# Order of two small products and of two vector steps in the second block of a two-block model

## What is computed

```
h_lat, h_ctx = rmsnorm(x) * (1 + sc1) + sh1, the same of ctx   # sh, sc, gt from silu(c) @ w_ada + b_ada
cols = h @ w_in                                                # latent attention, mLSTM, gates
q = rmsnorm(rmsnorm(c_q) @ w_uq); k, v from rmsnorm(c_kv) @ w_ukv   # 4 heads of 192, then a rotation
mla = softmax(q k^T * 192**-0.5) @ v                           # keys: 256 of ctx, then 256 of x
mlstm = both directions: sum over s of exp(level(t, s)) * (q.k) * v, divided by max(|den|, exp(-m))
x = x + gt1 * (concat(mla, mlstm) @ w_out)
h2 = rmsnorm(x) * (1 + sc2) + sh2
x = x + gt2 * peer(h2)     # 8 heads; top 16 of 128 x 128 experts each; gather rows, gelu(u.h2), weighted sum of v
```

## Time and profile before

| | us |
|---|---|
| three runs | 1439.12, 1436.99, 1438.72 |
| median | 1438.72 |
| the profiled execution: its own time | 1439.12 |
| its span, first to last instruction | 1437.8 |
| busy in it: TensorE, VectorE, ScalarE, GpSimd | 1028.5, 923.1, 357.8, 289.5 |

### The profile page before, as it was taken

The page is one execution under the profiler, slowest core; times in us unless marked ns, Lnnn a source line. Parts: engine busy times, 40 slices in busy tenths (PEclk is TensorE's granted clock), DMA queues, the critical chain, the costliest instruction groups (busy, mean ns, idle before and its releaser), DMA issues.

```text
span 1437.8 us, 17228 instructions
## 1 busy us (share of the span) xinstructions
PE 1028.5 (72%) x6241; PEld 596.9 (42%) x6241; DVE 923.1 (64%) x2448; ACT 357.8 (25%) x813; POOL 289.5 (20%) x265
## 2 busy tenths in 40 slices
PE   7997999999889999798777766764443444433434
PEld 4776655577665646344554422332111222211200
DVE  5487633438863536634457778788777676877665
ACT  2013523101353411364345432321111110101100
POOL 0000000000000000000033244445433434333441
PEclk9998999999899899898989889986666776655667
DMA  8462543445356242055069899999999999999997
GB/s 292 142 198 92 185 171 124 175 149 190 110 188 220 78 152 95 0 190 195 4 243 411 330 418 418 401 413 419 415 420 415 419 415 416 417 414 415 420 421 289
DMA packets 111927, 391.11 MB, mean 272 GB/s; under 512 B 10971, under 2 KB 39182, under 8 KB 79586
## 3 DMA queue, kind: packets, MB, share of 16 engines
q0 software_dynamic: 37440, 268.45, 45.3%
q1 hardware_dynamic: 74402, 121.56, 24.4%
HBM read 387.89 MB, written 1.05 MB: 271 GB/s over the span
## 4 chain that ended last, share of the span: by engine, by line
DMA 21%; DVE 18%; PE 14%; ACT 4%; POOL 3%; issue 3%; DVEq 0%; ACTq 0%
DMA e_uv<-in_experts_dram,e_listed 21%; PE bank L169 13%; DVE e_uv L2826 5%; POOL e_uv L3033 3%; ACT m_W L229 1%; DVE e_rest L2757 1%; DVE e_hot L185 1%; DVE e_diag L185 1%; ACT L229 1%; DVE e_si L2755 1%; DVE e_si L2761 1%; PE bank L174 1%; DVE m_W L185 1%; DVE e_sv L2759 1%; DVE e_sv L2753 1%
## 5 line engine op out<-in xcount | busy, mean ns | idle before, releaser
L3033 POOL DMA_INDIRECT e_uv<-in_experts_dram,e_listed x252 | 280.2, 1112 | 1112.1 <-DVE e_listed L202 835.7
L169 PE MATMUL bank<-e_uv,e_diag 128*32 128x512 f32 x1024 | 233.5, 887 | 321.5 <-DVE e_diag L185 321.2
L2826 DVE CUSTOM_DVE_ANT_0 e_uv<-e_uv,e_h2q 128x1024 f32<-128x1024 f32 x192 | 229.5, 1223 | 85.1 <-DMA e_uv<-in_experts_dram,e_listed 84.9
L169 PEld LDWEIGHTS bank<-e_uv,e_diag 128*32 128x32 f32 x1024 | 41.7, 140 | 448.4 <-DVE e_diag L185 364.4
L169 PE MATMUL bank<-hT,weights 128*128 128x256 f32 x640 | 145.9, 390 | 2.4 <-DVE hT L191 1.4
L169 PEld LDWEIGHTS bank<-hT,weights 128*128 128x128 f32 x640 | 124.3, 196 | 22.0 <-DVE hT L191 1.6
L229 ACT ACTIVATE e_act<-e_dot 128x4 f32<-128x4 f32 (+1 forms) x81 | 16.6, 205 | 393.1 <-DVE e_dot L2826 392.3
L229 ACT ACT_TABLE_LOAD x81 | 103.9, 1283 | 11.0 <-DVE e_dot L2826 2.9
L169 PE MATMUL bank<-weights,hT 128*128 128x512 f32 (+1 forms) x256 | 102.9, 558 | 2.3 <-DMA weights<-in_w_in_dram 2.3
L197 DVE SCALAR_TENSOR_TENSOR conv<-ubuf,vec,conv 128x256 f32<-128x256 f32 x240 | 96.8, 479 | 0.6
L2826 DVE CUSTOM_DVE_ANT_0 e_uv<-e_uv,e_hT 128x1024 f32<-128x1024 f32 x64 | 76.4, 1221 | 20.2 <-DMA e_uv<-in_experts_dram,e_listed 18.7
(11 more groups left out here) (384 smaller groups left out, 1432.1 us busy)
## 6 DMA issues: line engine op xcount, KB each, us to landing
weights<-in_w_in_dram SPq DMA_DIRECT2D x16, 2048.0 KB, 8.0
weights<-in_w_ada_dram SPq DMA_DIRECT2D x8, 2048.0 KB, 8.3
weights<-in_w_out_dram SPq DMA_DIRECT2D x6, 2048.0 KB, 7.8
e_w_pq<-in_w_pq_dram SPq DMA_DIRECT2D x12, 1024.0 KB, 26.3
weights<-in_cmp_w_dram SPq DMA_DIRECT2D x4, 2048.0 KB, 8.3
m_w<-in_w_in_dram SPq DMA_DIRECT2D x2, 2048.0 KB, 8.3
m_wo<-in_w_ada_dram SPq DMA_DIRECT2D x2, 2048.0 KB, 8.6
m_w<-in_w_ada_dram SPq DMA_DIRECT2D x2, 2048.0 KB, 10.3
```

Source lines behind the costliest of these rows:

```text
L169: ins = self.engine.matmul(out, lhsT, rhs, start=start, stop=stop, **kw)
L2826: dve.mark(c.nc.vector.tensor_tensor_reduce(u, u, h2q[tt][n], 1.0, 0.0, MUL, ADD, m["dot"][:, j:j + 1]), ("dots_set", g, c0) if n == c1 - ...
L3033: ins = c.nc.gpsimd.indirect_dma_start(out=to, out_offset=None, in_=rows, in_offset=bass.IndirectOffsetOnAxis(ap=of, axis=0))
```

## The change

The products `ada 5` and `ada 11` are issued behind `heads_turned` of their steps, no longer ahead. In the first tile, the softmax steps of head h+1 come behind the mLSTM steps on VectorE and ScalarE for every h; this changes the order at h = 0 and h = 2. No instruction is added or removed.

```
@@ mix_tensor
-        ahead = [work for work in HEAD_FILL[n] if n >= 5 and work[0] == "ada"]
-        for work in ahead:
-            fill(*work)
         if n:
             heads_turned(n - 1)
         for work in HEAD_FILL[n]:
-            if work not in ahead:
-                fill(*work)
+            fill(*work)
@@ mix_vector
         if h + 1 < MLA_H:
-            if h % 2 == 0:
-                t.att_max(h + 1)
             t.masked(h + 1)
-            if h % 2:
-                t.att_max(h + 1)
+            t.att_max(h + 1)
@@ mix_scalar
         if h + 1 < MLA_H:
-            if h % 2 == 0:
-                t.att_exp(h + 1)
             t.decays(h + 1)
-            if h % 2:
-                t.att_exp(h + 1)
+            t.att_exp(h + 1)
```

## The result

The changed kernel takes 1447.90 us (median of 5 runs, 1445.53 to 1449.19), the kernel before 1439.12 in the same comparison (5 runs). The ratio is 1.0052 with a 95% interval of 1.0034 to 1.0069, which is +7.5 us, from +4.9 to +9.9 (the two medians lie 8.8 apart, the two means 7.5). I had forecast +3.5, with a range up to 1446.2, and 1447.90 lies outside it. The sign was right, the size was half of what came, and one mechanism was missing.

What follows compares the result with a forecast made beforehand. The wait chain through 640 to 712 us to the first gather was taken to bound the kernel, one for one: 0.65 + 2.4 - 0.46 + 0.87 - 1.7 + 1.7 = +3.46 us, median 1442.2, range 1438.8 to 1446.2.

Steps and rivals of the forecast that it cites:

- step 5: Ada 5 behind its heads: longer TensorE idle time, then those heads at the low clock; +0.65 us, bounds 0 and 0.65.
- h = 0: First tile, head 0: the mask starts without waiting for VectorE's maximum, so ScalarE follows earlier; -0.46 us.
- Rival D: After the tile: the shift is absorbed, or matmuls pass each other; 1438.7 us, chance 0.03.
- C: Rival at h = 0 of the tile: shorter idle time removes the half-speed stretch; faster, -2.8 us, 1435.9, chance 0.08.
- A: Rival: the moved product alone costs, clock in the tile as before; +2.3 us, 1441.0, chance 0.33.
- h = 2: First tile, head 2: the exponential runs between decays and copy, so the copy TensorE waits for comes later; +0.87 us.
- a clock term of 1.7: At h = 2, ahead of 686.90: idle time grows from 1.47 to 2.34 us, bringing a short low stretch; +1.7 us.
- Ada 11: Behind the heads of step 6, uncovered on TensorE: 1.92 us at full clock, 3.84 at half; taken as +2.4 us.
- The clock at h = 0: Ahead of 669.36: shorter idle time may keep the clock high; -3.4 or 0, taken as -1.7 us.
- B: Rival: low clock lasts at steps 5 and 6 and h = 2; +8.3 us, 0.13 including what lies between it and forecast.

Runs made afterwards that it cites:

- experiment 4: The changed kernel, with the bank rotation skipping one bank at h = 2 so the transposes of head 2 take bank 7, not 6; +4.8 us against the kernel before.
- experiment 5: The kernel before with only ada 11 moved behind the heads of its step, ada 5 and the tile unchanged; +0.4 us (-1.0 to 1.9).
- experiment 6: The kernel before with the new order of softmax and mLSTM steps at h = 0 only; +0.4 us (-1.2 to 2.0).
- experiment 8: The kernel before with the new order at h = 0 and overwritten matmuls (6, 4 and 8) in three TensorE idle times; 1430.20 us against 1440.46, ratio 0.9931.
- experiment 10: The kernel before with 4 extra matmuls of constants ahead of TensorE's wait for the attention sum of head 0, nothing else; -3.0 us.

## Why the prediction was wrong in size

**Right.** The stretch sets the first gather and the first gather the end: counted from H5 the gather came 98.07 us later in place of 89.50, and G to end stayed within its spread. The moved ada 11 is uncovered, the idle time of step 5 is 3.73 (3.72 computed), the heads of step 6 came 9.23 us behind those of step 5 in place of 8.38, 0.85 more (0.65 said), h = 0 gave -0.44 (-0.46 said), and TensorE ran no matmul ahead of a waiting one. Rival D is out by the first gather (739.77), C by the low stretch at 670.90, and A by the time.

**The step that failed: h = 2.** "The copy comes 0.87 later, and TensorE waits for just that copy": it does not. It waits for `att_exp(3)` first, through bank 6. I had followed ScalarE's order to the copy, and given the bank exchanges of steps 5 and 6 their due, but not asked who waits for the exponential that I had moved. TensorE idled 3.80 us and came out of it at the low clock: +3.65 in length, against 0.87 and a clock term of 1.7. That these two add up to 2.57, near 3.65, is in part luck: the low stretch that the second stood for came from the bank's wait, and without that wait there was none (experiment 4).

**Mis-sized terms.** Ada 11: I took 2.4 between 1.92 and 3.84; H6 to L measured +3.20, since the low stretch of step 6 covered all of it. That is no independent term: experiment 5 has 2.0 where ada 5 stays ahead. The two moves act on each other through the clock. The clock at h = 0: I took -1.7 as the middle of -3.4 and 0, and got 0. Two outcomes far apart have no middle; with 0 the sum would have been +5.2. This is the largest miss in us. Of the 3.8 between 3.46 and 7.3 it is 1.7, h = 2 is 1.1, ada 11 is 0.8 and step 5 is 0.2. And X to G, 1.3 us longer, was no term at all. By terms, the sum of the first trace is 0.85 + 3.20 - 0.44 + 3.65 + 0 + 1.31 = 8.6, without the last one 7.3; whether that one reaches the end is open.

B had a size near the result (+8.3), and for it the low clock at steps 5 and 6 and at h = 2, but it lacked the bank, without which h = 2 keeps its clock (experiment 4). Its +8.3 came near by luck in that part.

## What to carry to other kernels

When an instruction that empties a buffer moves later, ask first who takes that buffer next: in a rotation of banks it can be work of another head, on another engine, ahead of the consumer that the data flow names. When work is moved out of an engine's idle time, the price is the work uncovered and also what the longer idle time does to the clock of what stands behind it. A few matmuls with no use in an idle stretch can be worth more than a better order.

## What the runs showed of the hardware

The granted clock behind an idle stretch is no matter of chance from one execution to the next here: in two executions of the kernel before and two of the changed kernel it fell or stayed at the same places from 640 to 730 us, to 0.02 us in the lengths. The Trainium skill, TensorE: Matmul & The Clock Gate, section What's actually happening, says that the same kernel can have different numbers of matmuls at the low clock from run to run; these two pairs of traces do not show that in this stretch, and here the measurement decides.

Idle time alone does not say whether the clock falls: 1.99 us ahead of V0 brought a fall (experiment 6), 2.33 us at h = 2 none (experiment 4). Nor does it say how long the low clock lasts: behind the same 4.19 us ahead of X it was about 6.8 us in five traces and about 10.2 in eight. Overwritten matmuls of constants kept it at 1.00 through 60 us (experiment 8). The same page, section HAM oscillation — how this bites in real kernels, advises, for thin products that wait for DMA, to restructure the loop so that the engine stays warm, or to pad the product. No run here does either, but the aim is the same, and the runs agree that it pays to keep the engine at the high clock: 3.0 us for four added matmuls (experiment 10), and 9.9 for eighteen with one exchanged order (experiment 8).
